# Each step of the state-space tiles at its own place among the groups of the first mixer

## What is computed

```python
y_conv = (cb * short_conv(cc * cx, conv_w[i])) @ w_conv_o[i]
ys = jax.nn.gelu(s5_ssm(u, ssm_a_re[i], ssm_a_im[i], ssm_b_re[i], ssm_b_im[i],
                        ssm_c_re[i], ssm_c_im[i], ssm_d[i], ssm_log_dt[i]))
...
# in s5_ssm:
lam_bar = jnp.exp(lam * dt)
b_bar = ((lam_bar - 1.0) / lam)[..., None] * b_c
bu = jnp.einsum("blgh,gph->blgp", uf.astype(jnp.complex64), b_bar)
_, states = lax.associative_scan(combine, (a_elems, bu), axis=1)
y = jnp.einsum("blgp,ghp->blgh", states, c_c).real
y = y + d.astype(jnp.float32).reshape(SSM_GROUPS, SSM_GROUP) * uf
```

## Time and profile before

| | |
|---|---|
| median of three runs | 3013.5 us |
| profiled execution, its own time | 3013.16 us |
| its span, first to last instruction | 3011.4 us |
| TensorE busy | 2675.7 us, 89% |
| VectorE busy | 1492.2 us, 50% |
| ScalarE busy | 904.9 us, 30% |
| GpSimd busy | 1115.2 us, 37% |
| mean granted clock of TensorE | 0.933 |
| mean HBM rate | 84 GB/s |

### The profile page before, as it was taken

How to read it: one execution, slowest core, us unless ns; L and a number is a source line. 1 busy time by engine, 2 the same in 40 slices (tenths; PEclk the granted TensorE clock), 3 DMA queues, 4 the chain that set the end, 5 groups by cost and what they waited for, 6 DMA issues and landing times. The chain is left out here.

```text
span 3011.4 us, 33078 instructions
## 1 busy us (share of the span) xinstructions
PE 2675.7 (89%) x12732; PEld 2114.9 (70%) x12732; DVE 1492.2 (50%) x1850; ACT 904.9 (30%) x1279; POOL 1115.2 (37%) x507
## 2 busy tenths in 40 slices
PE   5879999799996788999979999499998888599996
PEld 4657777688885566777768888377785667488884
DVE  6873434444443887344354443479825453533334
ACT  4222442222221322243132222234324432323221
POOL 3323333244341332333334343157941122243432
PEclk9989999899997898999989999699989988799998
DMA  4112222344332311222143343132221111132330
GB/s 152 49 43 81 77 74 67 99 134 135 115 118 66 99 50 50 88 70 78 42 148 119 121 139 101 48 114 83 77 77 43 42 35 56 57 105 84 99 96 35
DMA packets 226664, 253.42 MB, mean 84 GB/s; under 512 B 9072, under 2 KB 202992, under 8 KB 226288
## 3 DMA queue, kind: packets, MB, share of 16 engines
q1 hardware_dynamic: 226224, 251.30, 26.8%
q10 hardware_dynamic: 320, 0.52, 0.1%
HBM read 247.07 MB, written 4.19 MB: 83 GB/s over the span
## 5 line engine op out<-in xcount | busy, mean ns | idle before, releaser
L186 POOL TENSOR_TENSOR sb_w_lo<-sb_raw,sb_w_hi 128x1024 fp32r<-128x1024 f32 x404 | 977.4, 2434 | 1444.8 <-ACT sb_w_hi L181 1442.8
L181 ACT ACTIVATE sb_w_hi<-sb_raw 128x1024 fp32r<-128x1024 f32 x404 | 421.1, 1056 | 512.7 <-PE ps L207 448.5
L205 PE MATMUL ps<-sb_f_h_hi,sb_w_hi 128*128 128x512 f32 x960 | 384.9, 401 | 16.1 <-DVE sb_f_h_lo L1403 16.1
L206 PE MATMUL ps<-sb_f_h_lo,sb_w_hi 128*128 128x512 f32 x960 | 383.1, 399 | 0.0
L207 PE MATMUL ps<-sb_f_h_hi,sb_w_lo 128*128 128x512 f32 x960 | 382.6, 399 | 0.0
L205 PE MATMUL ps<-sb_h_hi,sb_w_hi 128*128 128x512 f32 x896 | 363.5, 406 | 18.4 <-DVE sb_h_lo L873 18.4
L206 PE MATMUL ps<-sb_h_lo,sb_w_hi 128*128 128x512 f32 x896 | 356.5, 398 | 0.0
L207 PE MATMUL ps<-sb_h_hi,sb_w_lo 128*128 128x512 f32 x896 | 356.2, 398 | 0.0
L205 PE MATMUL ps<-sb_f_hid_hi,sb_w_hi 128*128 128x512 f32 x608 | 244.6, 402 | 15.3 <-issue 7.5
L205 PE MATMUL ps<-sb_m_h_hi,sb_w_hi 128*128 128x512 f32 x576 | 242.7, 421 | 8.3 <-DVE sb_m_h_lo L1939 5.4
L207 PE MATMUL ps<-sb_f_hid_hi,sb_w_lo 128*128 128x512 f32 x608 | 243.8, 401 | 0.0
(11 more groups left out here) (324 smaller groups left out, 3667.9 us busy)
## 6 DMA issues: line engine op xcount, KB each, us to landing
sb_raw<-in_w_in_dram SPq DMA_DIRECT2D x148, 512.0 KB, 3.7
sb_raw<-in_w_ffn_in_dram SPq DMA_DIRECT2D x88, 512.0 KB, 5.8
sb_raw<-in_w_ff_dram SPq DMA_DIRECT2D x64, 512.0 KB, 3.7
sb_ada<-in_w_ada_dram SPq DMA_DIRECT2D x48, 512.0 KB, 4.4
sb_raw<-in_w_ffn_out_dram SPq DMA_DIRECT2D x44, 512.0 KB, 3.7
sb_raw<-in_w_mix_o_dram SPq DMA_DIRECT2D x16, 512.0 KB, 3.4
sb_raw<-in_w_conv_o_dram SPq DMA_DIRECT2D x8, 512.0 KB, 3.4
sb_raw<-in_w_attn_o_dram SPq DMA_DIRECT2D x8, 512.0 KB, 3.4
```

The costliest lines, as they stand in the source:

```text
L181: act.activation(w_hi[:, s, :], raw[:, s, :], ACT.Copy).then_inc(hi_done[s], 1)
L186: pool.tensor_tensor(w_lo[:, s, :], raw[:, s, :], w_hi[:, s, :].bitcast(F32), ALU.subtract)\
L205: pe.matmul(out, wh, hi, start=first and i == 0, stop=False)
L206: pe.matmul(out, wh, lo, start=False, stop=False)
```

## The change

Each step gets a table of its own, `{gi: ct}`. On TensorE `matrices` come one group later (3, 5, 7, 9), `inputs` at 4, 6, 8 and 11, and `outputs` of tiles 0, 1 and 3 in the middle of groups 6, 8 and 13, between the two units, while those of tile 2 stand behind group 10. VectorE's `b_matrices` move to 4, 6, 8, 10, `turns` and `c_matrices` of tiles 1 to 3 to 4, 6, 8, `states` to 5, 7, 9, 12, `gelu_start` to 6, 8, 11, 13, with `gelu_end` one group behind. ScalarE's `keep_lags` move to 5, 7, 9, 11, and `angles` and `sines` get places of their own. GpSimd's fractions follow the angles. The taps of `cx` 1 are taken one group later, behind `states(1)`. Two waits are new, both on `ssm_y`: `keep_lags(ct)` waits for the outputs of the tile before, and ScalarE's evacuation of `kv` waits for the outputs of all four tiles.

```diff
-        def ssm_step(gi, first):
-            ct, odd = divmod(gi - first, 2)
-            return ct if odd == 0 and 0 <= ct < SSM_TILES else None
-
-        MATRICES_AT, INPUTS_AT, STATES_AT, GELU_AT = 2, 3, 4, 5
+        MATRICES_AT = {3: 0, 5: 1, 7: 2, 9: 3}
+        INPUTS_AT = {4: 0, 6: 1, 8: 2, 11: 3}
+        MID_OUTPUTS_AT = {6: 0, 8: 1, 13: 3}
+        END_OUTPUTS_AT = {10: 2}
+        C_POWERS_AT = {4: 1, 6: 2, 8: 3}
+        B_POWERS_AT = {4: 0, 6: 1, 8: 2, 10: 3}
+        ANGLES_AT = {1: 0, 5: 1, 7: 2, 10: 3}
+        SINES_AT = {2: 0, 6: 1, 8: 2, 11: 3}
+        STATES_AT = {5: 0, 7: 1, 9: 2, 12: 3}
+        LAGS_AT = {5: 0, 7: 1, 9: 2, 11: 3}
+        GELU_AT = {6: 0, 8: 1, 11: 2, 13: 3}
...
-                        fractions_at.update({START1[STATES_AT + 2 * ct - 2] + AHEAD: ct for ct in range(1, SSM_TILES)})
+                        fractions_at.update({START1[gi] + AHEAD: ct for gi, ct in ANGLES_AT.items() if ct})
...
                                 if i == 0 and 1 <= a <= 8:
                                     values(a - 1)
-                            ct = ssm_step(gi, INPUTS_AT)
-                            if ct is not None:
-                                if ct == 0:
+                                if i == 0 and gi in MID_OUTPUTS_AT:
+                                    outputs(MID_OUTPUTS_AT[gi])
+                            if gi in INPUTS_AT:
+                                if INPUTS_AT[gi] == 0:
                                     emptied(pe, 0)
                                     emptied(pe, 1)
-                                inputs(ct)
-                            ct = ssm_step(gi, STATES_AT)
-                            if ct is not None:
-                                outputs(ct)
-                            ct = ssm_step(gi, MATRICES_AT)
-                            if ct is not None:
-                                if ct == 0:
+                                inputs(INPUTS_AT[gi])
+                            if gi in END_OUTPUTS_AT:
+                                outputs(END_OUTPUTS_AT[gi])
+                            if gi in MATRICES_AT:
+                                if MATRICES_AT[gi] == 0:
                                     pe.wait_ge(small_in, 8 * 16)
                                     pe.wait_ge(par_dve, 3)
-                                matrices(ct)
+                                matrices(MATRICES_AT[gi])
...
                             act.wait_ge(b_powers, ct + 1)
+                            if ct:
+                                act.wait_ge(ssm_y, ct)
...
+                            if gi in LAGS_AT:
+                                keep_lags(LAGS_AT[gi])
+                            if gi - 1 in GELU_AT:
+                                act.wait_ge(gelu_in, GELU_AT[gi - 1] + 1)
                                 act.activation(yw, yw, ACT.Tanh, scale=math.sqrt(2 / math.pi)).then_inc(gelu_th, 1)
                             prefetch(START1[gi] + 1 + AHEAD)
...
+                            if gi in ANGLES_AT:
+                                angles(ANGLES_AT[gi])
+                            if gi in SINES_AT:
+                                sines(SINES_AT[gi])
...
                                 if name == "kv":
+                                    act.wait_ge(ssm_y, SSM_TILES)
                                     step.done(act.activation(k[:, 0, :], src[:, 0, :], ACT.Copy))
...
+                            if gi in B_POWERS_AT:
+                                b_matrices(B_POWERS_AT[gi])
+                            if gi in GELU_AT:
+                                gelu_start(GELU_AT[gi])
+                            if gi in C_POWERS_AT:
+                                turns(C_POWERS_AT[gi])
+                                c_matrices(C_POWERS_AT[gi])
+                            if gi in STATES_AT:
+                                states(STATES_AT[gi])
+                            if gi == at1[("cx", 1)] + 1:
+                                short_conv(1)
+                            if gi - 1 in GELU_AT:
+                                gelu_end(GELU_AT[gi - 1])
...
-                                for i in range(2):
-                                    w = [pcol("conv_w", 4 * j + 2 * p + i) for j in range(3)]
...
+                                if p == 0:
+                                    short_conv(p)
```

More of the change, by code:

```diff
@@ L1069, in o_rest, with short_conv @@
                                        s_hi[r].bitcast(F32), ALU.subtract))
+                        def short_conv(p):
+                            for i in range(2):
+                                w = [pcol("conv_w", 4 * j + 2 * p + i) for j in range(3)]
+                                step.done(ts(conv[:, i, :], z[:, i, 0:T], w[0], None, ALU.mult))
+                                for j in (1, 2):
+                                    step.done(stt(conv[:, i, :], z[:, i, j:j + T], w[j], conv[:, i, :], ALU.mult, ALU.add))
                         pending = []
@@ L1083, in _ @@
                                 prod_rest(*pending.pop(0))
-                            ct = ssm_step(gi, INPUTS_AT)
-                            if ct is not None:
-                                b_matrices(ct)
-                            ct = ssm_step(gi, GELU_AT)
-                            if ct is not None:
-                                gelu_start(ct)
-                            ct = ssm_step(gi, MATRICES_AT - 1)
-                            if ct:
-                                turns(ct)
-                                c_matrices(ct)
-                            ct = ssm_step(gi, STATES_AT)
-                            if ct is not None:
-                                states(ct)
-                            ct = ssm_step(gi, GELU_AT + 1)
-                            if ct is not None:
-                                gelu_end(ct)
+                            if gi in B_POWERS_AT:
[11 more added lines that the diff above has]
+                                gelu_end(GELU_AT[gi - 1])
                             if gi == KV_AT + 3:
@@ L1116, in _ @@
                                 freed(tt(z[:, :, 2:], src, cc, ALU.mult))
-                                for i in range(2):
-                                    w = [pcol("conv_w", 4 * j + 2 * p + i) for j in range(3)]
-                                    step.done(ts(conv[:, i, :], z[:, i, 0:T], w[0], None, ALU.mult))
-                                    for j in (1, 2):
-                                        step.done(stt(conv[:, i, :], z[:, i, j:j + T], w[j], conv[:, i, :],
-                                                      ALU.mult, ALU.add))
+                                if p == 0:
+                                    short_conv(p)
                             elif name == "cb":
```

## The result

| | before | after |
|---|---|---|
| median of 4 runs each, us | 3013.61 (3012.50 to 3016.91) | 2946.04 (2943.54 to 2948.16) |
| ratio, 95% interval | | 0.9774 [0.9757, 0.9791] |
| profiled execution, its span, us | 3013.16, 3011.4 | 2946.3, 2944.5 |
| mean granted clock of TensorE | 0.933 | 0.941 |
| first rotation of pass 1, us | 282.83 | 250.05 |

67.6 us faster; the prediction was 53.2 faster, 2960 us, with a range of 2943 to 2984. The gain arises where it was looked for: 32.8 us up to the first rotation of pass 1, 66.2 up to that of pass 2, and 66.9 at the end.

What follows compares the result with a forecast made beforehand. TensorE and VectorE take turns: 38.4 us a pass to win on TensorE, less waits of 6.0, 1.4 and 3.2 and 1.2 of clock, gives 26.6, 53.2 in both passes: 3013.5 becomes 2960 us, range 2943 to 2984.

Steps and rivals of the forecast that it cites:

- the rival that has everything covered: `states` fast in every tile and no TensorE wait left: 38.4 us won a pass, 2937 us; chance 0.08, in part or whole.
- `matrices(0)` one group later: TensorE runs `cx` 0 first, so the wait of 7.34 us for `c_matrices(0)` is gone.
- Wait before `outputs(0)`: Tile 0: `states(0)` takes the slow 19.6 us and ends at 125.5, so TensorE waits 6.0 us (was 5.56).
- Tile 1: `states(1)` takes 14.0 us; wait 0 before `outputs(1)` (was 8.46); moving the `cx` 1 taps takes 4.2 us out of the path.
- New wait of `inputs(2)`: Tile 2: TensorE is ready at 171.7 and waits 1.4 us for the first operation of `gelu_start(1)`, ending at 173.1.
- Wait before `outputs(2)`: Tile 2: `states(2)` takes 16.6 us and ends at 199.5, TensorE comes at 196.3 and waits 3.2 us (was 11.30).
- `outputs(3)`: Tile 3: `states(3)` ends between 228.8 and 234.8, TensorE comes at 232.2; wait 0, between 0 and 2.6 (was 2.47).
- Later stages: Stages behind the changed stretch keep order and distances, so the gain should arrive whole at the end.
- Rival 4: Waits on `ssm_y` hold ScalarE's weight roundings past their 17 us of lead: 3078 us, slower; chance 0.05.
- Rival 1: GpSimd holds VectorE everywhere, 19.6 us for every `states`: only 15.4 us won a pass, 2983 us; chance 0.15.
- The reading of the scans: VectorE's `states` took 19.6 against 13.6 us because two GpSimd operations each hold one scan for 2.5 us.
- the clock: TensorE's waits cost 3.3 us of clock a pass before; after, 0.6 for one wait and 0.6 for cut groups.

Runs made afterwards that it cites:

- e6: Changed kernel with the taps of `cx` 1 put back ahead of `states(1)`: 2964.67 us, ratio 0.9835.
- e5: Changed kernel with `b_matrices(2)` right behind `states(1)` in group 7, ahead of the taps of `cx` 1: 2954.06 us, ratio 0.9798.
- e1: Changed kernel with `outputs` of tiles 0, 1 and 3 at the end of groups 6, 8 and 13, none in mid group: 2951.78 us, ratio 0.9790.
- e3: Changed kernel with its new distances but all steps one group earlier, taps in their old place: 2967.42 us, ratio 0.9837.
- e4: Changed kernel at an even pitch, `inputs(3)` in group 10 and all `outputs` in mid group 6, 8, 10, 12: 2965.13 us, ratio 0.9833.
- e8: Changed kernel with `b_matrices(2)` early, `outputs(0)` at the end of group 6 and `inputs(1)` in mid group 7: 2950.69 us, ratio 0.9787.
- e9: Changed kernel with `b_matrices(2)` early, `outputs(2)` at the end of group 11, angles and sine of tile 3 one group earlier: 2949.20 us, ratio 0.9793.
- e10: e9 with the last three operations of `gelu_start` behind the next tile's `states` for tiles 0 and 1: 2952.07 us, ratio 0.9813.
- e7: Changed kernel with GpSimd filling weight units 13 to 15 with zeros, reading nothing there, so computation is incomplete: 2932.53 us, ratio 0.9730.
- e11: Kernel before with only tile 3's inputs, states, outputs and gelu moved to their new places: 3009.26 us, ratio 0.9994.
- e2: Kernel before with every step one group later, at the old distances and with taps in their old place: 3029.53 us, ratio 1.0045.

## Why the prediction was right, and where its sizes were off

Right in mechanism and, within its range, in size; 6.2 us a pass short (26.6 against 32.8), on the side of the rival that has everything covered. By its own steps:

- **`matrices(0)` one group later**: right. L524 runs at 84.66 without a wait.
- **Wait before `outputs(0)`**: 6.0 predicted, 4.88 measured. The slow scans came as said, 11.79 us.
- **Tile 1**: wait 0, as said. `states(1)` took 13.9 us for a predicted 14.0. The place of the taps was worth more than the 4.2 us of their work (e6: 7.7).
- **New wait of `inputs(2)`**: 1.4 predicted, 1.29 measured, at the same operation. That the difference came out so near is in part luck: TensorE was ready at 170.56 and not at 171.7, and L1018 ended at 171.70 and not at 173.1.
- **Wait before `outputs(2)`**: 3.2 predicted, 0 measured. `states(2)` took 15.8 and not 16.6, and ended at 197.40, not 199.5; TensorE came at 198.09, not 196.3. It came late because of the lower clock behind the wait of 1.29. e5 takes that delay away, and the wait is there, 4.37 us. The prediction had the balance of the two engines nearly right (without the 3.1 us that the low clock cost, TensorE would have come at 195.0) and missed what a small wait ahead does to it.
- **`outputs(3)`**: wait 0, with 3.0 us to spare (225.98 against 229.02).
- **Later stages**: the gain arrives whole, 66.2 us at the second rotation and 66.9 at the end.
- **Rival 4** (ScalarE's queue): no wait of L205 for `w_lo` in the stretch.
- **Rival 1** (GpSimd holds VectorE everywhere): the mechanism is real and gives tile 0 its wait of 4.88, but the scans of tiles 1, 2 and 3 took 5.95, 3.63 and 5.64 us. In tile 2 two holds fell on the operations behind the scans (L1006, L1007) instead.
- **The reading of the scans**: the prediction put the slow `states` (19.6 against 13.6 us) down to two GpSimd operations of 2.5 us each. In the kernel before four of them fall among the slow scans, the two of L186 that it named and these:

```profile
142.56 2.40 POOL L489 TENSOR_TENSOR sb_ga<-sb_ga 128x1024 f32<-128x1024 f32 x1 [9.72 <-ACT sb_ga L697]
...
151.22 2.47 POOL L186 TENSOR_TENSOR sb_w_lo<-sb_raw,sb_w_hi 128x1024 fp32r<-128x1024 f32 x1 [1.32 <-ACT sb_w_hi L181]
```

Against free scans of 3.63 us each adds 2.0, and the quick row of 5.65 already holds one. The difference of 6.0 us that the sum used stands; a `states` without any hold would be 11.6 us, not 13.6.

- **The lower end of the range**: 2943 us is three quarters of the way from 2960 to 2937, not four fifths.

**The mis-sized terms are the wait before `outputs(2)` and the clock.** For the clock, I costed an undisturbed `outputs` at 5.8 us, from L547 at 3.99. That row was itself at a low clock: L553 without a wait takes 2.32, and `outputs` 4.1 (164.70 - 160.56). In the kernel before, L547 thus lost 1.7 + 2.3 + 2.3 + 1.8 = 8.1 us a pass where I saw 1.3 (its excess over 3.99). The granted clock fell to 0.50 in each of these four (116 to 118, 159 to 162, 205 to 210 and 239 to 241 us). With the 1.3 of `cx` 0 and some 0.6 of L552 that is about 10, not 3.3. For the same reason the sentence "the row of 3.99 speaks against it" was wrong; I had used the disturbed row as the yardstick. The Trainium skill (TensorE: Matmul & The Clock Gate, Part 1) has idle arrays fall to half rate; the trace agrees for each of these four waits and, as below, not for every wait.

The changed kernel loses 2.7 us at its wait of 4.88 (4.64 + 2.34 against 2.32 + 1.95), and 3.1 at the wait of 1.29: `inputs(2)` takes 5.36 us and not 4.17, the unit behind it 7.80 (177.13 to 184.93) and not the 5.86 of the one before it. I had charged 1.2 for both and the cuts of groups.

**The account of a pass.** Waits: 35.1 before, 6.2 after, 28.9 won (24.5 predicted). Start of the stretch: 0.3. The rest, 32.8 - 28.9 - 0.3 = 3.6, is clock: about 10 lost before, 5.8 after, 0.6 unassigned (2.1 net predicted). The miss of 6.2 is then 4.4 in waits (3.2 of it at `outputs(2)`), 0.3 and 1.5.

**What bounds it now.** In 72 to 250 us TensorE works 171.6 of 178 us, so its own work is most of the stretch; 6.2 us of waits and 5.8 of clock are all that is left to win there in a pass with TensorE's work as it is. These waits hang on VectorE's chain: it is 150.5 to 154.7 us in the changed kernel and in e1, e3, e4, e5, e8, e9 and e10, wherever the waits were put. e5, e8, e9 and e10 each removed a wait that showed and got it back elsewhere; e7, which shortened VectorE's work itself, brought 13 to 16 us by the ratios. But the chain alone doesn't rank the orders: e3 and e4 have chains of 151.0 and 151.8 us and take 2967 and 2965. The first rotation stands at the end of the chain plus what TensorE still does behind it, and that was 45.3 us before, 34.0 in e3 and e4, and 24.1 in the changed kernel. The gain of 32.8 is 11.6 from an earlier end and 21.2 from the shorter rest, and e11 shows that the second is not to be had without the right order of tiles 0 to 2 (rest 24.1, chain 181.4). Differences of a few us between orders also hold the luck of the clock: the same wait of 2.04 us behind the rotation left it at 1.00 in both passes of the changed kernel and of e9, and halved it for some us in both passes of e5 and e8.

By the difference of held and free durations of the same operation, over all rows of the stretch, GpSimd's reads cost VectorE about 33 us of the 153 (30 before the change). That is a sum worked out from one trace, and only the part in e7 was tried. Why the shift alone lengthens the chain by 12 us (e2) stays open.

## What to carry to other kernels

When two engines wait for each other in turns, removing one wait moves it; first give the longest step of the slower engine its full length of the other's work as cover. Ask of each new order when the whole chain of the slower engine ends and how much work of the faster one stands behind that end, not where the waits show. Take the undisturbed duration of an operation from an occurrence without a wait in front, in this kernel or in another stage, before subtracting: a row behind a wait already holds the loss one is looking for. A short independent operation (here the taps, 4.2 us) ahead of the critical step cost nearly twice its length (7.7 us), as it also caught the other engine's interference.

## What the runs showed of the hardware

- **A short wait may halve the clock, or not.** 1.29 us of standing in the changed kernel: granted 0.77 over the next 15 us, 0.50 in the middle of them, 3.1 us lost. 1.28 us before the same group in the first pass of e7: clock 1.00 and L544's counterpart at 0.94 us; 1.29 us there in the second pass of e7: 0.77 again. 2.04 us before the same products: 1.00 in the changed kernel, 0.62 in e8. Neither the length of the wait nor the order of the work around it decides alone; what does stays open. A forecast can only bound this, here by 0 to 3 us a wait.
- **GpSimd holds more than scans.** VectorE's L1074 has one tile in SBUF and a column of factors, writes to SBUF, and took 2.55 us at 84.75 against 0.49 free. L1006, two inputs in SBUF and its output in PSUM, took 3.41 against 1.23. The Trainium skill (SBUF — State Buffer, Who interferes with whom) tells of VectorE instructions with two SBUF inputs; L1006 agrees. The same section lists `tensor_scalar` among those that can contend, in modes that use two ports; L1074 agrees, though no run shows its mode.
- **Writing alone doesn't hold.** Two memsets of GpSimd, 1.84 us together, lay among the scans of tile 0 in e7. These took 5.76 us, what scans with one reading operation among them cost (5.64 in tile 3 of the changed kernel).
